# A decoder layer in one kernel: last stores awaited at the next write of their buffers instead of at the stage borders

## The chip, the cores and the metric

The kernel runs on one core of a Trainium2 chip. The metric is the device time of one execution in microseconds, as the median over several runs. The profile comes from one execution of its own. Engine names are those of the profile: PE is TensorE (PEld its weight loads), DVE VectorE, ACT ScalarE, POOL GpSimd, SP the engine that issues most DMAs.

## The reference

One step of a decoder layer, all in float32, for 2048 prompt tokens and 8 sequences of 8 decode tokens (17 tiles of 128 tokens). Cut to what matters here:

```python
mod = silu(c) @ w_ada + b_ada                       # sh1, sc1, gt1, sh2, sc2, gt2
hn = rms_norm(x, g_pre_mix) * (1 + sc1) + sh1
u, q, k, v = split(hn @ w_in, [512, 1024, 1152])    # 512 | 512 | 128 | 128 columns
attn = attn_prompt(q, k, v, sinks, table)           # window 128, 8 heads, 2 kv heads, one sink per head
ssm_y, h_last = s5_scan(u, lam, log_dt, b, c, d)    # 32 groups of 16 channels, complex state of 64
z = gelu(ssm_y); ssm_out = z * sigmoid(z @ w_glu + b_glu)
mixed = concat(rms_norm(ssm_out), rms_norm(attn)) @ w_out
x = x + gt1 * rms_norm(mixed, g_post_mix)
hn2 = rms_norm(x, g_pre_ffn) * (1 + sc2) + sh2
x = x + gt2 * rms_norm(hier_moe(hn2), g_post_ffn)   # top 1 of 4 groups, top 2 of 4 experts
```

The decode tokens run the same with cached keys and values and a given scan state. The outputs are `x`, the last 128 keys and values, and the scan's last states, for both kinds of tokens.

## The kernel before, in words

`hybrid_layer` runs five stages in order. **front** computes the first two modulations and the projection `x @ w_in` for 17 tiles and stores each to `scratch_proj` (`store`, L250 to 252, the counters `stored[0]` for even tiles and `stored[1]` for odd ones); beside it the scan's matrices are built and stored to `scratch_rec` (`store_rec`). Tile 16 (`LAST`) holds the decode tokens and is even. **s5** runs the scan for 32 groups `g`: SP loads each group's matrices into a ring of four (`load_rec`), `u` and `us` (the decode tokens') come from `scratch_proj`, PE, DVE, ACT and POOL work a group in a fixed order of steps (`contribute`, `back`, `unflip` on PE), and `y` goes to `scratch_y` in quarters (`store_y`). Beside the groups runs the second half of the modulation, `modulate(n)` for n of 0 to 15 on PE with `w_ada` loaded by `load_w(n)`, finished by DVE in two parts, `folded` 1 at g = 17 and `folded` 2 behind the last group. Its rows go to `scratch_mods` (`store_rows`, four DMAs from SP, four from ACT), the last states to four outputs (`store_states`, three DMAs from each). **attention** works the tiles in `ORDER`: 0 to 5, the decode tokens "S", 6 to 15, with `q` and `k` in two buffers `held_qk` (tiles 0 and 1 are loaded during s5; `load(t)` waits until tile t - 2 is flipped). Meanwhile POOL runs `MixingWeights.split` (L1299): 48 loads of the modulation's rows for the decode tokens (`mw_mod<-scratch_mods`), then it splits ten weight tiles in two parts for the next stage. **mixing** does gate, norms, output projection and residual for 17 tiles; its SP stores `x` and `hn` and, for each tile, fills one tile of `scratch_acc` with zeros (`clear(t)`, 18 in all). **moe** runs the experts and adds their results into `scratch_acc`.

Every stage is a `with Stage(...)`: its SBUF and PSUM tiles and one block in which each engine has its own instruction list. Orders are written out by hand; there is no planner. At a block's end all five engines meet (their instructions have line L79). Before it, SP (in s5 ACT's list ends with stores too) waits in the old kernel for every store of the stage: in front L326 to 329, in s5 L1049 and L1050 (`stored`, 24 DMAs), in attention L1403, in mixing L1814 to 1817. Buffers of a stage share addresses with those of the next, so a store must have been read out before the next stage writes there.

Semaphores are held by a `Semaphores` object. Its exit is a barrier of all engines (L64), a clear of its counters by POOL (L65) and a second barrier (L66). In the old kernel there are three such groups: front with s5, attention with mixing, and moe. So the first exit stands between s5 and attention.

Of the kernel before, what the change touches and what calls it, by code (L numbers as in the profile page):

```python
# [22 lines left out]
P = 128  # L23
# [14 lines left out]
L = 8  # L38
# [10 lines left out]
class Semaphores:  # L49
# [12 lines left out]

    def __exit__(self, *a):
        self.nc.all_engine_barrier()  # L64
        self.nc.clear_and_free_semaphores(self.held)  # L65
        self.nc.all_engine_barrier()  # L66
# [94 lines left out]
def front(nc, T, top, cT):  # L161

    with Stage(nc, top, "fr") as s:
# [79 lines left out]
        def _(sp):  # L243
# [81 lines left out]
            sp.wait_ge(stored[0], 9 * 16)  # L325
# [209 lines left out]
        def _(dve):  # L535
# [278 lines left out]
            for t in range(NT):  # L814
# [18 lines left out]
                if t == 0:  # L833
                    power_tables()

# [59 lines left out]
class AttentionFirst:  # L895


    def __init__(self, held):
        sb = held.sb
        self.ident, self.sink, self.bias = sb("ident", [P, P]), sb("sink", [P, NH]), sb("bias", [P, NH, 2 * WIN])  # L900
        self.qk = sb("qk", [P, 2, AW + KVW])
        self.arrived, self.kv_stored = held.sem("first"), held.sem("kv_stored")
# [21 lines left out]

U5 = 4


def s5(nc, T, top, cT, first):

    with Stage(nc, top, "s5") as s:  # L930
        ident, swap = first.ident, s.sb("swap", [P, P])
        u, us = s.sb("u", [P, 2, L, SW]), s.sb("us", [DB, L, SW])
        y, ys = s.sb("y", [P, 2, L, SW]), s.sb("ys", [DB, L, SW])
# [8 lines left out]
        fin, fins = s.sb("fin", [NG, P]), s.sb("fins", [P, 2, P])  # L942
        w, mod, gains = s.sb("w", [P, 2, 2048]), s.sb("mod", [P, 2, 512]), s.sb("gains", [P, 2, 512])
# [8 lines left out]
        last_ready, edges, fin_mm, fin_out, stored = (s.sem(n) for n in ("last_ready", "edges", "fin_mm", "fin_out", "stored"))  # L952
# [7 lines left out]
        yp = T["y"][0:SEQ, :].rearrange("(i p j) c -> p i j c", i=2, j=L)  # L960
        ysv = T["y"][SEQ:SEQ + NS, :].rearrange("(b j) c -> b j c", j=L)
# [9 lines left out]

        def store_rows(eng, h):
            for n, row in enumerate((2, 4)):
                a = n * 2 + h
                eng.dma_start(T["mods"][:, row, h * 512:(h + 1) * 512], mod[32 * a:32 * a + NRW, 0, :]).then_inc(stored, 16)
            for a in (2 * h, 2 * h + 1):
                eng.dma_start(T["mods"][:, 3, a * 256:(a + 1) * 256], mod[32 * a:32 * a + NRW, 1, 0:256]).then_inc(stored, 16)

        def store_states(eng, r):
            part, c = ("re", "im")[r], slice(r * NST, (r + 1) * NST)  # L980
            eng.wait_ge(fin_out, 2)
            eng.dma_start(T[f"o_ssm_{part}_prompt"][0, 0], fin[:, c]).then_inc(stored, 16)
            for n in range(2):
                dst = T[f"o_ssm_{part}_sample"].rearrange("a b g p -> (a b g) p")[n * P:(n + 1) * P, :]
                eng.dma_start(dst, fins[:, n, c]).then_inc(stored, 16)

        @blk.sync
        def _(sp):
# [17 lines left out]
            def store_y(b):  # L1006
                sp.wait_ge(y_out, (b + 1) * 8)
                c = slice(b * CB, (b + 1) * CB)
                for i in range(2):
                    sp.dma_start(yp[:, i, :, c], y[:, i, :, c]).then_inc(stored, 16)  # L1010
# [16 lines left out]
            sp.dma_start(T["cT"], cT[:, :, :].rearrange("p k n -> p (k n)")).then_inc(stored, 16)  # L1027
            for g in range(U5, NG):
# [14 lines left out]
            sp.wait_ge(y_out, NG)  # L1043
            sp.dma_start(ysv, ys[:, :, :]).then_inc(stored, 16)
            store_y(3)
            sp.wait_ge(folded, 2)
            store_rows(sp, 0)
            store_states(sp, 0)
            first.finish(sp)  # L1049
            sp.wait_ge(stored, 24 * 16)  # L1050

        @blk.scalar
        def _(act):
# [39 lines left out]
            act.wait_ge(folded, 2)  # L1093
            store_rows(act, 1)
            store_states(act, 1)

        @blk.tensor
        def _(pe):
# [39 lines left out]

            def modulate(n):
# [14 lines left out]
            for g in range(NG):  # L1154
# [8 lines left out]
            pe.wait_ge(mod_done, 2)  # L1163
            pe.wait_ge(edges, 1)
            pe.wait_ge(tail_in, 3 * 16)
            nc.tensor.matmul(ps_f[0:NG, 0:P], lastA[:, :], ident[:, :], start=True, stop=False)
            nc.tensor.matmul(ps_f[0:NG, 0:P], lastB[:, :], swap[:, :], start=False, stop=True)
            for n in range(2):
                last = nc.tensor.transpose(ps_f[:, (n + 1) * P:(n + 2) * P], ss[:, 4 * n:4 * n + 4, :].rearrange("q b g -> q (b g)"), ident[:, :])
            last.then_inc(fin_mm, 1)  # L1170
# [26 lines left out]
        def _(dve):  # L1197
# [53 lines left out]
            modulation(1)  # L1251
            vec.scalar_tensor_tensor(mod[:, 1, 0:256], mod[:, 1, 0:256], 1.0, gains[:, 1, 0:256], ALU.add, ALU.mult).then_inc(folded, 1)
# [5 lines left out]
            vec.tensor_copy(fin[:, :], ps_f[0:NG, 0:P]).then_inc(fin_out, 1)  # L1258
            vec.tensor_copy(fins[:, :, :], ps_f[:, P:3 * P].rearrange("p (n q) -> p n q", n=2)).then_inc(fin_out, 1)
# [4 lines left out]
class MixingWeights:  # L1264
# [34 lines left out]
    def split(self, nc, pool, T):  # L1299

        nc.gpsimd.memset(self.w_rt[:, :, NR:], 0.0).then_inc(self.padded, 1)
# [1497 lines left out]
```

## Time and profile before

| | us |
|---|---|
| median of 3 runs | 1610.88 (1610.49 to 1613.52) |
| the profiled execution | 1611.89 |
| its span | 1610.1 |
| front | 0 to 355.9 |
| s5 | 355.9 to 511.8 |
| attention | 511.8 to 675.4 |
| mixing | 675.4 to 1018.8 |
| moe | 1018.8 to the end |

The stage borders are the first instructions of each stage in the timeline. Over the span PE is busy 84%, DVE 74%, ACT 45% and POOL 33% of the time, and the mean granted clock of PE is 0.92 of full speed. A timeline row gives start, busy time, engine, line, operation and tiles, the count of instructions merged in it, and in brackets how long the engine stood idle before and what released it. SPq, ACTq and PEq are the sequencers of these engines: their rows are DMA issues and waits.

### The profile page before, as it was taken

Reading aid. Unit: us, or ns where it says so; the run is one execution under the profiler, and the core shown is the slowest. Engines: PE = TensorE matmul, PEld = TensorE weight load, DVE = VectorE, ACT = ScalarE, POOL = GpSimd, SP = SyncE. Lnnn points to the kernel's source line nnn. Section 1 sums busy time; section 2 is a strip of 40 time slices with the busy share of each in tenths; the row PEclk is TensorE's granted clock in tenths of the full one; section 3 lists DMA queues with packets and bytes.
Section 4 is the critical chain, followed back from the end, with each engine's and each line's share of the span. In section 5 each row is a group of like instructions: output and inputs, shape, how many; then the busy total and the mean of one; then the engine's idle time right before and its main releaser. Section 6 shows DMA issues by size and latency. Waiting matters only on the chain. (4 is left out here: it accounts for less than half of the span.)

```text
span 1610.1 us, 24720 instructions
## 1 busy us (share of the span) xinstructions
PE 1352.4 (84%) x7108; PEld 1029.4 (64%) x7109; DVE 1185.6 (74%) x2154; ACT 729.7 (45%) x1564; POOL 537.9 (33%) x719
## 2 busy tenths in 40 slices
PE   4899989979996879689999997179999999999910
PEld 1687777856664546467777775157777777777700
DVE  3799898846684767546666664668899888988738
ACT  2321212102342737533444342137777777777633
POOL 1105567642223860012112211134444444444300
PEclk8899999987997979889999998579999999999965
DMA  9412434449986642214433442875788888885597
GB/s 344 144 69 104 156 124 162 178 162 364 333 273 164 193 147 85 100 39 162 163 132 130 158 155 92 280 254 111 198 230 251 261 217 242 250 212 123 114 311 292
DMA packets 139063, 301.08 MB, mean 187 GB/s; under 512 B 22312, under 2 KB 79913, under 8 KB 136246
## 3 DMA queue, kind: packets, MB, share of 16 engines
q1 hardware_dynamic: 110742, 221.06, 39.8%
q0 software_dynamic: 20800, 61.13, 16.4%
q10 hardware_dynamic: 7448, 17.99, 3.2%
q8 instruction: 36, 0.59, 0.2%
q14 instruction: 37, 0.30, 0.1%
HBM read 317.05 MB, written 103.70 MB: 261 GB/s over the span
## 5 line engine op out<-in xcount | busy, mean ns | idle before, releaser
L2569 DVE TENSOR_TENSOR ex_w_lo<-ex_wgu,ex_w_hi 128x1024 fp32r<-128x1024 f32 x192 | 226.2, 1221 | 46.8 <-ACT ex_w_hi L2366 46.6
L2366 ACT ACTIVATE ex_w_hi<-ex_wgu 128x1024 fp32r (+1 forms) x192 | 192.4, 1055 | 42.7 <-issue 23.0
L2329 POOL DMA_INDIRECT scratch_acc<-ex_o,ex_to x48 | 95.9, 1999 | 253.6 <-DVE ex_o L2599 184.1
L116 PE MATMUL ex_ps_h<-ex_w_hi,ex_xT 128*128 128x512 f32 x384 | 156.3, 407 | 2.7 <-DVE ex_x_lo L2563 2.7
L116 PE MATMUL fr_ps_m<-fr_whi,fr_hl 128*128 128x512 f32 (+1 forms) x408 | 150.6, 369 | 7.3 <-DVE fr_io L598 4.4
L118 PE MATMUL ex_ps_h<-ex_w_hi,ex_x_lo 128*128 128x512 f32 x384 | 151.8, 395 | 0.0
L117 PE MATMUL ex_ps_h<-ex_w_lo,ex_xT 128*128 128x512 f32 x384 | 151.1, 393 | 0.0
L117 PE MATMUL fr_ps_m<-fr_wlo,fr_hl 128*128 128x512 f32 (+1 forms) x408 | 148.1, 363 | 0.0
L118 PE MATMUL fr_ps_m<-fr_whi,fr_hl 128*128 128x512 f32 (+1 forms) x408 | 147.5, 361 | 0.0
L1828 POOL TENSOR_SCALAR mx_st<-mx_st 128x1 f32<-128x1 f32 x68 | 29.4, 433 | 267.1 <-ACT mx_j L1872 151.4
L116 PE MATMUL mx_ps_m<-mw_hi,mx_hT 128*128 128x512 f32 x272 | 108.0, 397 | 4.1 <-issue 2.1
L117 PE MATMUL mx_ps_m<-mw_lo,mx_hT 128*128 128x512 f32 x272 | 106.7, 392 | 0.0
L118 PE MATMUL mx_ps_m<-mw_hi,mx_h_lo 128*128 128x512 f32 x272 | 106.6, 392 | 0.0
L2698 PE MATMUL ex_ps_o<-ex_wd,ex_aT 128*128 x192 | 98.0, 591 | 0.0
L116 PEld LDWEIGHTS fr_ps_m<-fr_whi,fr_hl 128*128 128x128 f32 x408 | 79.1, 194 | 22.9 <-DVE fr_io L598 5.3
L118 PEld LDWEIGHTS fr_ps_m<-fr_whi,fr_hl 128*128 128x128 f32 x408 | 79.4, 195 | 11.8
L117 PEld LDWEIGHTS fr_ps_m<-fr_wlo,fr_hl 128*128 128x128 f32 x408 | 79.5, 195 | 11.4
L116 PEld LDWEIGHTS ex_ps_h<-ex_w_hi,ex_xT 128*128 128x128 f32 x384 | 73.2, 191 | 17.2 <-DVE ex_x_lo L2563 2.4
L118 PEld LDWEIGHTS ex_ps_h<-ex_w_hi,ex_x_lo 128*128 128x128 f32 x384 | 72.9, 190 | 16.4
L117 PEld LDWEIGHTS ex_ps_h<-ex_w_lo,ex_xT 128*128 128x128 f32 x384 | 73.5, 191 | 14.2
L409 ACT ACTIVATE fr_hl<-fr_ps_t 128x512 fp32r<-128x512 f32 x34 | 18.5, 595 | 131.0 <-PE fr_ps_t L471 121.2
L1437 ACT ACTIVATE at_sc<-at_sc,at_nm 128x256 f32<-128x256 f32 (+1 forms) x128 | 62.7, 493 | 17.7 <-DVE at_nm L1513 17.7
(454 smaller groups left out, 3388.0 us busy)
## 6 DMA issues: line engine op xcount, KB each, us to landing
ex_wgu<-in_w_exp_gate_dram SPq DMA_DIRECT2D x51, 1024.0 KB, 11.8
ex_wgu<-in_w_exp_up_dram SPq DMA_DIRECT2D x51, 1024.0 KB, 14.7
ex_wd<-in_w_exp_down_dram SPq DMA_DIRECT2D x51, 1024.0 KB, 11.1
scratch_rec<-fr_w SPq DMA_DIRECT2D x16, 1112.0 KB, 5.4
s_rec<-scratch_rec SPq DMA_DIRECT2D x32, 556.0 KB, 6.3
scratch_proj<-fr_io SPq DMA_DIRECT2D x17, 640.0 KB, 3.0
scratch_acc<-in_zeros_dram SPq DMA_DIRECT2D x18, 512.0 KB, 6.0
scratch_x<-mx_x SPq DMA_DIRECT2D x17, 512.0 KB, 2.7
```

The lines of the kernel that those rows point to most:

```text
L116: nc.tensor.matmul(out, hi, w_hi, start=first, stop=False)
L117: nc.tensor.matmul(out, hi, w_lo, start=False, stop=False)
L118: return nc.tensor.matmul(out, lo, w_hi, start=False, stop=final)
L409: A(hi[:, t % 2, 4 * h:4 * h + 4, :], ps_t[:, h, :].rearrange("p (k n) -> p k n", k=4), ACT.Copy).then_inc(moved_a, 1)
L1437: last = A(sc[:, p % 2, h, k0:], sc[:, p % 2, h, k0:], ACT.Exp, bias=nm[:, p % 2, h:h + 1], accum_out=sm[:, p % 2, h:h + 1])
L1828: last = nc.gpsimd.tensor_scalar(a[:, col + m:col + m + 1], a[:, col + m:col + m + 1], c, EPS, ALU.mult, ALU.add)
L2329: pool.indirect_dma_start(T["acc"], bass.IndirectOffsetOnAxis(to[:, t:t + 1], 0), o[:, t % 2, :], None, compute_op=ALU.add).then_inc(sem(" ...
L2366: A(w_hi[:, par, c * PW:(c + 1) * PW], wgu[:, bass.ds(slot * (KD * 2 * DE) + c * PW, PW)], ACT.Copy).then_inc(S["w_rounded"], 1)
L2569: vec.tensor_tensor(w_lo[:, par, c * PW:(c + 1) * PW], wgu[:, bass.ds(slot * (KD * 2 * DE) + c * PW, PW)], w_hi[:, par, c * PW:(c + 1) * P ...
L2698: last = nc.tensor.matmul(ps_o[:, at], aT[:, 1, :], wd[:, bass.ds((slot * 2 + 1) * D + c * 512, 512)], start=False, stop=True)
```

## The change

- **Front** no longer waits for the last even store (`stored[0]` 8 instead of 9 DMAs). s5 makes that wait before it loads `us`, which now comes behind `load_u(0)`.
- **s5**: an object `ScanResults` holds the tiles that are stored late, with one counter `scan_stored`. Four of the stores of modulation rows (the two rows that are complete at `folded` 1) are issued by SP at g = 21. The four matmuls for the last states come before the last `unflip` on PE and write to `s_ps_s`, and DVE takes them before its last modulation part. The thirteen stores at the stage's end are gone from both lists; SP waits only for `cT` and the cache copies.
- **Attention**: SP issues these thirteen behind `v` and tile 2, which moves up. POOL waits for all 23 before it writes the weights' tiles. POOL clears the counters of front and s5 behind its first two weight loads, without barriers.
- **Attention to mixing**: the last odd tile's store is awaited in mixing, by SP ahead of its loop and by ACT.
- **Mixing**: the zero fills `clear(LAST)` and `clear(NT)` come ahead of the loop.
- Counters: `early` (front, s5) and `late` (attention, mixing, and the held ones) instead of one group per pair of stages.

```diff
@@ Semaphores
+    def clear(self):
+        self.nc.clear_and_free_semaphores(self.held)
...
@@ front, SP
-            sp.wait_ge(stored[0], 9 * 16)
+            sp.wait_ge(stored[0], 8 * 16)
@@ ScanResults
+    def store_gate_and_shift(self, sp, T):
+        for n, row in enumerate((2, 4)):
+            for h in range(2):
+                a = n * 2 + h
+                sp.dma_start(T["mods"][:, row, h * 512:(h + 1) * 512], self.mod[32 * a:32 * a + NRW, 0, :]).then_inc(self.stored, 16)
+
+    def store_rest(self, sp, T):
+        for a in range(4):
+            sp.dma_start(T["mods"][:, 3, a * 256:(a + 1) * 256], self.mod[32 * a:32 * a + NRW, 1, 0:256]).then_inc(self.stored, 16)
+        self.store_y(sp, T, 3)
+        sp.dma_start(T["y"][SEQ:SEQ + NS, :].rearrange("(b j) c -> b j c", j=L), self.ys[:, :, :]).then_inc(self.stored, 16)
+        for r, part in enumerate(("re", "im")):
...
+    def all_stored(self, eng):
+        eng.wait_ge(self.stored, 23 * 16)
@@ s5, SP
-            sp.dma_start(us[:, :, :], usv).then_inc(loaded, 16)
             sp.dma_start(ident[:, :], T["ident"]).then_inc(loaded, 16)
             load_u(0)
+            sp.wait_ge(proj_stored, (NT // 2 + 1) * 16)
+            sp.dma_start(us[:, :, :], usv).then_inc(loaded, 16)
...
+                if g == 21:
+                    sp.wait_ge(folded, 1)
+                    res.store_gate_and_shift(sp, T)
...
-            sp.wait_ge(y_out, NG)
-            sp.dma_start(ysv, ys[:, :, :]).then_inc(stored, 16)
-            store_y(3)
-            sp.wait_ge(folded, 2)
-            store_rows(sp, 0)
-            store_states(sp, 0)
+            sp.wait_ge(cT_out, 16)
             first.finish(sp)
-            sp.wait_ge(stored, 24 * 16)
@@ s5, ACT
-            act.wait_ge(folded, 2)
-            store_rows(act, 1)
-            store_states(act, 1)
@@ s5, PE
+                if g == NG - 1:
+                    last_states()
                 unflip(g)
@@ MixingWeights.split, POOL
+        first.results.all_stored(pool)
         nc.gpsimd.memset(self.w_rt[:, :, NR:], 0.0).then_inc(self.padded, 1)
...
         self.load_raw(pool, T, 1)
+        early.clear()
@@ attention, SP
             sp.dma_start(v[:, :, :], pv[:, 0:NPT, AW + KVW:]).then_inc(v_in, 16)
+            load(2)
+            first.results.store_rest(sp, T)
...
-                sp.wait_ge(tile_out[t], NPT // 2 * 16)
+                sp.wait_ge(tile_out[t], (NPT // 2 - t) * 16)
@@ mixing, SP
+            clear(LAST)
+            clear(NT)
+            sp.wait_ge(m.attn_stored, NPT // 2 * 16)
             run(sp, step, HALF - 2)
             store(Tile(0, LAST))
             sp.wait_ge(S["kept"], 32)
-            clear(LAST)
-            clear(NT)
@@ mixing, ACT
             round_z(Tile(0, 0))
+            act.wait_ge(m.attn_stored, NPT // 2 * 16)
             square_attn(Tile(0, 0))
@@ hybrid_layer
+        with Semaphores(nc) as late, Stage(nc, late, "held") as held:
...
+            proj_stored = front(nc, T, early, cT)
...
+                attention(nc, T, late, mw, first, early)
+                mixing(nc, T, late, mw, lg)
```

How the lists move at three places. SP from the end of s5 to the start of attention, before (`s_` tiles are s5's, `at_` attention's; L79 is the border):

```order
L1044 DMA scratch_y<-s_ys 8x4096
L1010 DMA scratch_y<-s_y 1024x1x128 x2
L975 DMA scratch_mods<-s_mod 9x512 x2
L977 DMA scratch_mods<-s_mod 9x256 x2
L982 DMA out_ssm_re_prompt_dram<-s_fin 32x64
L985 DMA out_ssm_re_sample_dram<-s_fins 128x64 x2
L79 UNCONDITIONAL_BRANCH
L1360 UNCONDITIONAL_BRANCH
L1374 DMA at_v<-scratch_proj 128x16x128
L1376 DMA at_s_hsel<-in_hsel_dram 8x256
L1377 DMA at_s_sink_c<-in_attn_sinks_dram 8x1
L1378 DMA at_s_qkv<-scratch_proj 64x768
```

and with the change (the border is L83 now):

```order
L83 UNCONDITIONAL_BRANCH
L1384 UNCONDITIONAL_BRANCH
L1398 DMA at_v<-scratch_proj 128x16x128
L1388 DMA held_qk<-scratch_proj 128x640
L954 DMA scratch_mods<-s_mod 9x256 x4
L944 DMA scratch_y<-s_y 1024x1x128 x2
L956 DMA scratch_y<-s_ys 8x4096
L959 DMA out_ssm_re_prompt_dram<-s_fin 32x64
L962 DMA out_ssm_re_sample_dram<-s_fins 128x64 x2
L959 DMA out_ssm_im_prompt_dram<-s_fin 32x64
L962 DMA out_ssm_im_sample_dram<-s_fins 128x64 x2
L1402 DMA at_s_hsel<-in_hsel_dram 8x256
```

The stage's stores stand behind the border, and tile 2 ahead of them. PE at the end of s5, before:

```order
L1127 MATMUL s_ps_v<-s_B,s_rec 128x256
L1130 MATMUL s_ps_v<-s_A,s_rec 128x264
L1136 MATMUL s_ps_y<-held_ident,s_yT 128x128 x2
L1137 MATMUL s_ps_y<-held_ident,s_yT 8x128
L1147 MATMUL s_ps_f<-s_w,held_cT 32x256 x4
L1166 MATMUL s_ps_f<-held_ident,s_lastA 32x128
L1167 MATMUL s_ps_f<-s_swap,s_lastB 32x128
L1169 MATMUL s_ps_f<-held_ident,s_ss 128x128 x2
L79 UNCONDITIONAL_BRANCH
```

and with the change:

```order
L1145 MATMUL s_ps_v<-s_B,s_rec 128x256
L1148 MATMUL s_ps_v<-s_A,s_rec 128x264
L1160 MATMUL s_ps_s<-held_ident,s_lastA 32x128
L1161 MATMUL s_ps_s<-s_swap,s_lastB 32x128
L1163 MATMUL s_ps_s<-held_ident,s_ss 128x128 x2
L1154 MATMUL s_ps_y<-held_ident,s_yT 128x128 x2
L1155 MATMUL s_ps_y<-held_ident,s_yT 8x128
L1174 MATMUL s_ps_f<-s_w,held_cT 32x256 x4
L83 UNCONDITIONAL_BRANCH
```

The products with `s_lastA`, `s_lastB` and `s_ss` no longer follow the modulation (`s_w`) but precede the last unflip. POOL at the start of attention, before (the two ISA rows, L65 in both, are the clears of counters):

```order
L79 UNCONDITIONAL_BRANCH
L65 ISA
L1405 UNCONDITIONAL_BRANCH
L1301 MEMSET mw_w_rt 128x8x12
L131 DMA mw_mod<-scratch_mods 8x1024 x48
L1295 DMA at_raw<-in_w_glu_dram 128x2x512 x2
```

and with the change:

```order
L83 UNCONDITIONAL_BRANCH
L1430 UNCONDITIONAL_BRANCH
L1323 MEMSET mw_w_rt 128x8x12
L135 DMA mw_mod<-scratch_mods 8x1024 x48
L1316 DMA at_raw<-in_w_glu_dram 128x2x512 x2
L65 ISA x2
```

The clear leaves the border and stands behind the first weight loads.

## Rows read from the trace of the kernel before

**Rows 1.** Windows: stretch, us, busy of each engine (instructions), clock, DMA share, GB/s.
```profile
500.00:512.00 12.00, 1.17 (x7) 0.79 (x8) 1.49 (x5) 0.00 (x0) 0.18 (x1) 0.63 0.49 120
512.00:525.00 13.00, 9.49 (x53) 6.83 (x53) 4.90 (x31) 6.27 (x22) 12.77 (x25) 0.68 1.00 223
```
**Rows 2.** SP's waits, 330 to 372 us: total, times, longest.
```profile
SPq L79 <- DMA scratch_proj<-fr_io: 1.4, 1, 1.4
```
**Rows 3.** Timeline, start of s5.
```profile
365.20 0.42 ACT L1062 ACTIVATE s_ug<-s_u 128x256 f32<-128x256 f32 x1 [22.12 <-DMA s_u<-scratch_proj]
...
369.31 0.69 PE L1108 MATMUL s_ps_u<-held_ident,s_ug 128*128 128x128 f32 x2
```
**Rows 4.** Timeline, s5 around the ring load of group 22.
```profile
449.70 1.31 SPq L1010 DMA_DIRECT2D scratch_y<-s_y  x2
...
451.92 2.87 SPq L992 DMA_DIRECT2D s_rec<-scratch_rec  x1
...
459.68 0.68 PE L1118 MATMUL s_ps_s<-s_uT,s_rec 128*128 128x264 f32 x2 [0.88 <-issue]
```
**Rows 5.** Timeline, end of s5 and first product of attention.
```profile
498.78 0.64 PE L1147 MATMUL s_ps_f<-s_w,held_cT 128*32 128x256 f32 x8
...
499.44 0.30 SPq L1044 DMA_DIRECT2D scratch_y<-s_ys  x1
...
499.95 0.42 DVE L1252 SCALAR_TENSOR_TENSOR s_mod<-s_mod,s_gains 128x256 f32<-128x256 f32 x1
...
500.40 0.55 ACTq L975 DMA_DIRECT2D scratch_mods<-s_mod  x1
...
502.02 0.40 DVE L1259 COPY s_fins<-s_ps_f 128x256 f32<-128x256 f32 x1
...
505.51 0.97 ACTq L985 DMA_DIRECT2D out_ssm_im_sample_dram<-s_fins  x2
...
506.32 0.93 SPq L985 DMA_DIRECT2D out_ssm_re_sample_dram<-s_fins  x2
...
511.80 1.09 PE L1577 MATMUL at_ps_q<-held_ident,held_qk 128*128 128x128 f32 x4 [10.02 <-PEq L66]
```
**Rows 6.** Lines L1050 and L65: count, ns min/median/max, first and last start.
```profile
L1050 SPq EVENT_SEMAPHORE  x1: 28/28/28, 509.4 to 509.4; - x1
...
L65 POOLq EVENT_SEMAPHORE_RANGE_CLEAR  x3: 524/591/657, 510.5 to 1609.2; - x3
```
**Rows 7.** DMA issues, 512 to 540 us: count, KB each, median us from issue to landing.
```profile
held_qk<-scratch_proj SPq DMA_DIRECT2D x4, 320.0 KB, 8.5
```
**Rows 8.** Timeline, attention's first tiles (SP's loads of tiles 3 and 4, PE's first products).
```profile
518.80 0.34 SPq L1364 DMA_DIRECT2D held_qk<-scratch_proj  x1
...
524.21 0.63 PE L1577 MATMUL at_ps_q<-held_ident,held_qk 128*128 128x128 f32 x4 [0.73 <-DMA held_qk<-scratch_proj]
...
529.79 0.58 SPq L1364 DMA_DIRECT2D held_qk<-scratch_proj  x1
...
530.83 0.44 PE L1577 MATMUL at_ps_q<-held_ident,held_qk 128*128 128x128 f32 x2
...
538.52 0.66 PE L1577 MATMUL at_ps_q<-held_ident,held_qk 128*128 128x128 f32 x4
```
**Rows 9.** PE's granted clock at attention's start (window of PE), and POOL's first row of mixing.
```profile
512.00:513.00 1.00, 1.00 (x5) 0.50 0.09 28
...
675.44 0.10 POOL L1819 MEMSET mx_half<- 128x2 f32 x1 [83.01 <-POOLq L79]
```
**Rows 10.** Line L1403, SP's last wait of attention.
```profile
L1403 SPq EVENT_SEMAPHORE  x1: 1628/1628/1628, 673.4 to 673.4; - x1
```
**Rows 11.** SP's waits, 1000 to 1030 us, and the timeline's last row of mixing.
```profile
SPq L79 <- DMA scratch_acc<-in_zeros_dram: 2.7, 1, 2.7
SPq L1814 <- DMA scratch_hn<-mx_hn: 2.1, 1, 2.1
...
1014.55 0.18 DVE L1986 TENSOR_TENSOR kept_lg<-mx_ps_g,mw_b_rt 128x20 f32<-128x20 f32 x1 [2.22 <-PE mx_ps_g L2092]
```

More of the change, by code:

```diff
@@ L61, in get @@
         return self.held[-1]
+    def clear(self):
+        self.nc.clear_and_free_semaphores(self.held)
     def __exit__(self, *a):
         self.nc.all_engine_barrier()
-        self.nc.clear_and_free_semaphores(self.held)
+        self.clear()
         self.nc.all_engine_barrier()
@@ L834, in _ @@
                     power_tables()
+        return stored[0]
 BW = 3 * WIN
@@ L901, in __init__ @@
         self.qk = sb("qk", [P, 2, AW + KVW])
-        self.arrived, self.kv_stored = held.sem("first"), held.sem("kv_stored")
+        self.arrived, self.kv_stored, self.scan_stored = held.sem("first"), held.sem("kv_stored"), held.sem("scan_stored")
     def load_tiles(self, sp, T):
@@ L970, in cols @@
             return slice(g * GC, (g + 1) * GC)
[L972 to L985, printed above, removed]
         @blk.sync
@@ L1137, in unflip, with last_states @@
                 nc.tensor.transpose(ps_y[0:DB, 2 * P:3 * P], yT[:, g % 2, NCH:], ident[:, :]).then_inc(y_flipped, 1)
+            def last_states():
+                pe.wait_ge(edges, 1)
+                pe.wait_ge(tail_in, 3 * 16)
+                nc.tensor.matmul(ps_s[0:NG, 0, 0:P], lastA[:, :], ident[:, :], start=True, stop=False)
+                nc.tensor.matmul(ps_s[0:NG, 0, 0:P], lastB[:, :], swap[:, :], start=False, stop=True)
+                for n in range(2):
+                    last = nc.tensor.transpose(ps_s[:, 0, (n + 1) * P:(n + 2) * P], ss[:, 4 * n:4 * n + 4, :].rearrange("q b g -> q (b g)"), ident[:, :])
+                last.then_inc(fin_mm, 1)
             def modulate(n):
@@ L1162, in _ @@
                     modulate(g // 2)
[L1163 to L1170, printed above, removed]
         @blk.gpsimd
@@ L1297, in load_raw, with split @@
             pool.dma_start(dst, T["w_out"][0, (k - 2) * P:(k - 1) * P, :]).then_inc(arrived, 16)
-    def split(self, nc, pool, T):
+    def split(self, nc, pool, T, first, early):
+        first.results.all_stored(pool)
         nc.gpsimd.memset(self.w_rt[:, :, NR:], 0.0).then_inc(self.padded, 1)
@@ L1324, with attention @@
 HEADS = [[kv * GQ + 2 * half + g for kv in range(NKV) for g in range(2)] for half in range(2)]
-def attention(nc, T, top, mw, first):
+def attention(nc, T, top, mw, first, early):
     NB = 2 * NKV
@@ L1379, in _ @@
             sp.dma_start(s_vn[:, :, :], new[:, SW + AW + KVW:].rearrange("(b t) c -> t b c", t=DT)).then_inc(s_loaded, 16)
-            load(2)
             for kv in range(NKV):
@@ L1406, in _ @@
         def _(pool):
-            mw.split(nc, pool, T)
+            mw.split(nc, pool, T, first, early)
         @blk.scalar
@@ L2752, in hybrid_layer @@
         T[name] = nc.dram_tensor(f"scratch_{name}", shape, dt).ap()
+    early = Semaphores(nc)
     with Stage(nc, None, "kept") as kept:
         lg = kept.sb("lg", [P, NT, NR])
-        with Stage(nc, None, "held") as held:
-            with Semaphores(nc) as top:
-                held.top = top
-                cT = held.sb("cT", [P, KD, 32])
-                front(nc, T, top, cT)
-                first = AttentionFirst(held)
-                first.spare = cT
-                s5(nc, T, top, cT, first)
-            with Semaphores(nc) as top:
-                with Stage(nc, top, "mw") as weights:
-                    mw = MixingWeights(weights)
-                    attention(nc, T, top, mw, first)
-                    mixing(nc, T, top, mw, lg)
+        with Semaphores(nc) as late, Stage(nc, late, "held") as held:
+            cT = held.sb("cT", [P, KD, 32])
+            proj_stored = front(nc, T, early, cT)
+            first = AttentionFirst(held)
+            first.spare = cT
+            s5(nc, T, early, cT, first, proj_stored)
+            with Stage(nc, late, "mw") as weights:
+                mw = MixingWeights(weights)
+                attention(nc, T, late, mw, first, early)
+                mixing(nc, T, late, mw, lg)
         with Semaphores(nc) as top:
```

45 lines of the change are left out of this document (29 added, 16 removed).

## The prediction

> **What bounds it now.** The printed chain of waits reaches back only into the last stage, so the borders had to be read one by one. First the windows [rows 1] show where the program stands still: in 500 to 512 us PE works 1.17 us of 12 and the DMA engines are half busy; the 13 us behind it have the DMA engines at 1.00 and 223 GB/s. Then the queue engine's own waits show which border waits for what [rows 2, 6, 10, 11], and the timeline shows what stands ahead of each border and behind it. Four places count: front to s5 (A), s5 to attention (B), attention to mixing (C), mixing to the experts (D).
>
> **A, minus 1.35.** Once the scan matrices' stores have landed, SP ends front with 1.4 us more for the last store of the projection [rows 2]. The second wait goes. It is made again in s5 behind the first load of `u`, some 2 us after the border; by then the 1.4 us have run out, so it should be met on arrival. The load of `us` behind it comes about 1 us later. Its readers: ACT gathers `u` and `us` from 365.20 (until 365.8), PE flips the first group only at 369.31, after the bias products [rows 3]. Some 3.5 us cover it. Bounds: 1.2 to 1.4.
>
> **s5 at g = 21, plus 0.5.** Four stores of 18 KB now stand on SP ahead of the ring load for group 22. SP waited there with 0.9 us to spare (its store of `y` was done at 451.01, the ring load went out at 451.92), and four issues at 0.33 (the quick ones of its queue) are 1.3. So the load goes out 0.4 late, and PE is already short of it: 0.88 us idle at 459.68, whose cause the row does not name [rows 4]. At the pace of the same stores at the stage's end (0.55 for the first of them, [rows 5], over 1 for the others) it would be 2, if the ring makes it up it is 0.
>
> **B, minus 10.7.** Last real work before it: PE's modulation ends at 499.42, DVE's fold at 500.37, then the last states on PE and two copies until 502.42. The stores run from 499.44 to 507.25 on SP (ten) and from 500.40 to 506.48 on ACT (seven) [rows 5]. SP's wait for them ends at 509.4, and the barrier, 0.657 us clear, barrier bring PE's first attention product to 511.80 [rows 5, 6]. In the changed program the states come before the last unflip, so DVE's fold ends the stage. PE's unflip moves by four small matmuls, of which part lies in PE's waits: 0.3, so DVE ends near 500.65. Stage A's own rendezvous took about 0.4 from the last branch to the first instruction. Attention starts near 501.05: 511.75 less that is 10.7. If the modulation waits for the copies too it is 10.0, if unflip does not move it is 11.1. Nothing of what was waited for sits on PE's path: the first two tiles were loaded during s5.
>
> **The start of attention, plus 1.6.** The stores don't vanish, they go into SP's list behind `v` and tile 2. Before, counted from attention's first instruction (SP's at 511.75, just ahead of PE's in [rows 5]), tile 3's load was issued at +7.05 and wanted at +19.1, tile 4's issued at +18.0 and wanted at +26.8; such a load landed in 8.5 [rows 7, 8]. Thirteen more issues, eleven at 0.35 and the two halves of `y` at 0.65 [rows 4], are 5.2, so tile 3 goes out at +12.2 and lands at +20.7: **1.6 late**. Tile 4's load stands behind three copies that wait for the eight bias loads; it moves by 0 to 5.2. At 0 it lands at +26.5 and is in time, at 5.2 it lands at +31.7, when the want has itself moved to +28.4: 3.3 late; I take the middle, **1.7**, because both ends have a reason. For the early one: POOL waits for all 23 stores before its 48 loads of 32 KB (1.5 MB), which before began at once and filled the queues [rows 1]. Sum of stalls 3.3; the ends are 0 (rival 1) and those of rivals 2 and 3. Against that stands the clock: at the stage's start the granted clock was 0.50, level 1.2 GHz, after PE's 10.02 us of idle [rows 5, 9]; without that idle I expect the 2.4 GHz level. Four transposes took 1.09 at the low level and 0.63 later [rows 5, 8]. The first 13 us hold some four such groups' worth of transposes, 0.46 each: **minus 1.7** (0 if the clock falls all the same; 9.49 busy us at 0.68 [rows 1] give 3.0 at most). That is plus 1.6.
>
> What hides the rest: POOL's weights were done 83.0 us before mixing wanted POOL [rows 9], and the wait for the stores costs it some 15. The two clears on POOL now lie inside attention and cost 1.1 of that same cover. Without it they would be 1.1 on the path.
>
> **C, minus 1.6.** SP's wait for the last attention store was 1.628 us [rows 10]; now only the even tiles are awaited, which have landed. Who reads it next is mixing, and there both new waits come later than the store's landing, 1.6 us after SP's issue: SP's stands behind eleven issues at the stage's start, and ACT's ahead of the first square of the attention half, which cannot start before that tile's own loads are in. The two zero fills moved ahead of the loop meet an SP that is idle for some 16 us before its next load at 696.4. Cost nothing; 0.5 if they slow the loads under way.
>
> **D, minus 1.1.** SP's last wait was for the second zero fill: 2.7 us, of which the `hn` store ahead had run out 2.1 us into its own wait [rows 11]. With the fills moved, the stage ends with DVE at 1014.73 or the `hn` store at 1014.3, not at 1017.0 [rows 11]: minus 2.2. But the counters of this group lie apart now and the clear is three instructions for one. A clear takes 0.591 us in the median [rows 6], 0.55 as the two extra ones follow without a drain: plus 1.1, on the path, for every engine stands at the second barrier. **The end, plus 1.1:** the last group's clear also falls into three. Bounds of both: 0, if the clears pipeline, to 1.3.
>
> **Sum.** −1.35 + 0.5 − 10.7 + 1.6 − 1.6 − 1.1 + 1.1 = −11.55. The profiled execution took 1611.89 (span 1610.1), so 1600.3; it stood 1.0 above the median of the runs, 1610.88, so 1599.3 on their scale. I round to **1599.0**.
>
> **Rival 1, no stall at all (17%).** SP issues at 0.35 and the queues stay short since POOL holds back: tile 3 lands in 6, not 8.5, tile 2, issued 3.5 us earlier, removes the 0.73 wait for it [rows 8], and the clock stays up. Then −13.15 for the terms outside attention, −1.7 and −0.7: −15.55, 1595. For it: POOL's 1.5 MB are gone from the crowded stretch. Against it: the DMA share there was 1.00 and the stores bring 1.3 MB (two halves of 0.52, `ys` 0.13, the states 0.15).
>
> **Rival 2, the loads stand behind the stores' bytes (15%).** 1.3 MB at the 223 GB/s of that stretch are 5.8 us. If tile 3 lands in 8.5 + 5.8 instead of 8.5, it comes at +26.5, 7.4 late, and with tile 4's 1.7 the stalls are 9.1 instead of 3.3: −5.75, 1605. What would do it here: the queue serves what was issued first. The Trainium skill (DMA: Bandwidth & Descriptors, "Queues, rings and completion order") says so of the counter: its increment lands only after every earlier write of that DMA engine, across its queues. By that rule alone the time would be rival 2's. The trace does not settle it: 8.5 us for 320 KB behind 1 MB of `v` [rows 7] fits the rule and mere sharing alike.
>
> **Rival 3, slower (4%).** SP issues the stores as slowly as the stage's end did, when they took 7.8 on SP and 6.1 on ACT at once [rows 5]: 13.9 in one list, and SP works alone now. Tile 3 goes out at +21, lands at +29.5, 10.4 late, and tile 4 another 3.3. PE stands still each time and comes back at 0.50: two tiles at some 2 us more. 17.7 in all against −13.15 of the other terms: plus 4.5, 1615. It decides once attention's start is worse by over 16.3. Against it: the slow issues were two engines' at once and with full queues; single ones on SP take 0.30 to 0.34 [rows 5, 8].
>
> **Rival 4, it doesn't do what it says (4%).** Another wait ends last at B (SP's for the cache copies, POOL's or ACT's branch) and most of the 10.7 comes back: 1608 to 1611, within 0.2%.
>
> **Numbers.** 0.2%, about what a measurement of this kernel can tell, is 3.2 us. The forecast has 60%, its own terms reach from −17 to −8. The range takes in rivals 1 and 2: 1594 to 1606. Slower by over 0.2% is rival 3, 4%; the same is rival 4 and a corner of rival 2 with slow issues, 6%; the rest, 90%, is faster.
>
> **What would show it.** A: s5's first instruction at about 354.6, and no wait of SP for the projection in s5. B: attention's first product near 499 to 500 on the new scale, less than 1 us of PE idle ahead of it, a granted clock of 1.00 in its first us. Tile 3's load issued at about +12 and PE waiting for it 1 to 2 us; SP issuing thirteen stores in 4 to 7 us. POOL starting its 48 loads some 14 us into attention, done with 60 us to spare. C: mixing starts within 0.5 us of the last attention store's issue. D: three clears in a row, 1.7 us. The forecast is wrong if PE waits over 5 us for tile 3 or 4, if attention (163.6 us before) gets longer by over 4, or if s5's groups behind 21 run slower.

## The result, and the profile after

The changed kernel took 1592.57 us in the median of 4 runs (1590.79 to 1596.33), the kernel before 1610.68 in its 4; the ratio is 0.9894, with a 95% interval from 0.9869 to 0.9918. That is 18.1 us (13.2 to 21.1) where 12 were forecast, and 1592.57 lies below the range. In a later comparison of the same two kernels (after_again, below) the ratio was 0.9884 (0.9854 to 0.9915).

The profiled execution of the changed kernel took 1590.79 us, 21.1 less than the one before. By stage, from the first instruction of each:

| | before | after | difference | forecast |
|---|---|---|---|---|
| front, up to its last projection store | 351.24 | 348.85 | −2.4 | 0 |
| that store to s5's first load (A) | 4.68 | 3.37 | −1.3 | −1.35 |
| s5, first load to DVE's last fold | 144.03 | 146.72 | +2.7 | +0.8 |
| that fold to attention's first load (B) | 11.80 | 0.71 | −11.1 | −11.0 |
| attention, first load to the last at_o | 160.51 | 154.79 | −5.7 | +1.6 |
| at_o to mixing's first operation (C) | 3.18 | 1.58 | −1.6 | −1.6 |
| mixing, up to its last logits | 339.11 | 340.74 | +1.6 | 0 |
| logits to the experts' first load (D) | 4.26 | 2.13 | −2.1 | −1.1 |
| the experts, to the span's end | 591.29 | 590.11 | −1.2 | +1.1 |

The borders did what they were meant to do. Front's −2.4 is the luck of two profiles: over all that were taken its means are 350.3 us with the old borders (six) and 350.1 with the new ones (eight). The page's head:

```profile
span 1589.0 us, 24710 instructions
...
PE 1350.5 (85%) x7108; PEld 1029.8 (65%) x7109; DVE 1176.2 (74%) x2154; ACT 728.7 (46%) x1564; POOL 534.7 (34%) x719
```

The same 2154 instructions of DVE are busy 1176.2 us instead of 1185.6. Nothing in the change should make DVE faster; that is the first trace of what the forecast had missed.

The timeline around B and the first tiles, which answers to [rows 5] and [rows 8]:

```profile
498.94 0.42 DVE L1280 SCALAR_TENSOR_TENSOR s_mod<-s_mod,s_gains 128x256 f32<-128x256 f32 x1
499.65 0.38 SPq L1398 DMA_DIRECT2D at_v<-scratch_proj  x1
...
499.69 0.63 PE L1602 MATMUL at_ps_q<-held_ident,held_qk 128*128 128x128 f32 x4 [1.27 <-PEq L83]
...
502.04 1.61 SPq L954 DMA_DIRECT2D scratch_mods<-s_mod  x4
...
503.69 1.26 SPq L944 DMA_DIRECT2D scratch_y<-s_y  x2
505.00 1.83 SPq L956 DMA_DIRECT2D scratch_y<-s_ys  x1
...
509.93 0.89 SPq L962 DMA_DIRECT2D out_ssm_im_sample_dram<-s_fins  x2
...
515.73 0.35 SPq L1388 DMA_DIRECT2D held_qk<-scratch_proj  x1
...
520.06 0.92 PE L1602 MATMUL at_ps_q<-held_ident,held_qk 128*128 128x128 f32 x4 [3.71 <-DMA held_qk<-scratch_proj]
...
521.15 0.58 SPq L1388 DMA_DIRECT2D held_qk<-scratch_proj  x1
```

PE is idle 1.27 us at the border where it was 10.02, and its first four transposes take 0.63 us where they took 1.09. Thirteen stores take SP from 502.04 to 510.82, 8.8 us and not 5.2, so tile 3's load goes out at +16.1 (forecast +12.2); but it lands in 4.3 us, not 8.5, and PE starts on it at +20.4 after 3.71 us of waiting. The window of PE that answers to [rows 9], and the two wide ones that answer to [rows 1] (500 to 513 and 513 to 526):

```profile
500.00:501.00 1.00, 0.42 (x4) 1.00 0.15 30
```
```profile
500.00:513.00 13.00, 9.01 (x62) 5.84 (x60) 5.68 (x34) 8.82 (x31) 1.01 (x3) 0.87 0.78 215
513.00:526.00 13.00, 9.29 (x61) 6.69 (x61) 6.45 (x30) 6.60 (x24) 13.00 (x27) 0.87 0.90 214
```

The granted clock is at full speed in attention's second us. The DMA share is 0.78 where it was 1.00, and POOL, whose loads filled that stretch before, has hardly begun (fifth pair: 1.01 us busy). The counters' clears, which answer to [rows 6], and SP's waits before D, which answer to [rows 11]:

```profile
L65 POOLq EVENT_SEMAPHORE_RANGE_CLEAR  x8: 46/254/415, 538.4 to 1588.5; - x8
```
```profile
SPq L1840 <- DMA scratch_hn<-mx_hn: 3.5, 1, 3.5
```

Eight clears have a median of 0.254 us, where three had 0.591. The wait for a zero fill is gone; SP's last one there is for the store of `hn`.

### The profile page after: what moved, and what is told of

Read it like the earlier page. It is cut to its first block and busy times, and to the rows that moved or that the text cites. A ratio compares the mean times of both kernels' runs of the same rounds, so it can differ in the third digit from the quotient of the medians.

```text
span 1589.0 us, 24710 instructions
## 1 busy us (share of the span) xinstructions
PE 1350.5 (85%) x7108; PEld 1029.8 (65%) x7109; DVE 1176.2 (74%) x2154; ACT 728.7 (46%) x1564; POOL 534.7 (34%) x719
## 5 line engine op out<-in xcount | busy, mean ns | idle before, releaser
L2349 POOL DMA_INDIRECT ex_x<-scratch_hn,ex_rows x48 | 52.4, 1092 | 52.5 <-DVE ex_rows L2569 25.6
```

The lines of the kernel that those rows point to most:

```text
L2349: pool.indirect_dma_start(x[:, t % U, :], None, T["hn2"], bass.IndirectOffsetOnAxis(rows[:, t:t + 1], 0)).then_inc(S["x", t % U], 16)
```

## What made attention shorter

DVE's groups in attention, kernel before and after (line, operation, shape, count, busy us, mean ns, idle before). Before:

```profile
L1513 DVE SCALAR_TENSOR_TENSOR at_nm<-at_mx,at_nsink 128x4 f32<-128x4 f32 x32 | 8.5, 266 | 1.1
L1532 DVE TENSOR_TENSOR at_sm<-at_sm,at_es 128x8 f32<-128x8 f32 x16 | 7.2, 451 | 0.0
...
L1502 DVE SCALAR_TENSOR_TENSOR at_nm<-at_mx,at_s_nsink 128x2 f32<-128x2 f32 x2 | 2.5, 1264 | 0.2
L1493 DVE TENSOR_SCALAR at_s_nsink<-at_s_sink 128x4 f32<-128x4 f32 x1 | 2.3, 2304 | 0.0
```

After:

```profile
L1538 DVE SCALAR_TENSOR_TENSOR at_nm<-at_mx,at_nsink 128x4 f32<-128x4 f32 x32 | 7.1, 223 | 1.1
...
L1557 DVE TENSOR_TENSOR at_sm<-at_sm,at_es 128x8 f32<-128x8 f32 x16 | 3.5, 219 | 0.0
L1527 DVE SCALAR_TENSOR_TENSOR at_nm<-at_mx,at_s_nsink 128x2 f32<-128x2 f32 x2 | 2.7, 1372 | 0.2
...
L1518 DVE TENSOR_SCALAR at_s_nsink<-at_s_sink 128x4 f32<-128x4 f32 x1 | 0.2, 171 | 0.0
```

Operations of 2 to 8 columns take 0.16 us, and now and then over 2. One such meeting, in the timeline of the kernel before, and the same operation in that of the changed one:

```profile
562.26 2.35 POOL L1310 TENSOR_TENSOR mw_lo<-at_raw,mw_hi 128x1024 fp32r<-128x1024 f32 x1
562.37 2.26 DVE L1532 TENSOR_TENSOR at_sm<-at_sm,at_es 128x8 f32<-128x8 f32 x1
```
```profile
550.70 0.30 DVE L1557 TENSOR_TENSOR at_sm<-at_sm,at_es 128x8 f32<-128x8 f32 x1
...
551.05 2.36 POOL L1333 TENSOR_TENSOR mw_lo<-at_raw,mw_hi 128x1024 fp32r<-128x1024 f32 x1
```

The small one of DVE starts 0.11 us after POOL's subtraction and ends with it, at 564.6. In the changed kernel's profile the subtraction starts 0.05 us behind the end of DVE's. That need not be the change's doing: in a second profile of the kernel before (before_again, below) the same operation took 0.24 us. I call **excess** what the small operations of DVE in attention (`at_nm`, `at_sm`, `at_ds`, `at_s_nsink`) take above 0.162 us each: 13.9 us before, 5.4 after. The difference, 8.5, is close to what attention lost from tile 5's first product (at +34.24 before, at +36.81 after) to the start of its last `at_o`: 126.3 and 118.0, so 8.3. (The expectations below count attention to the end of that `at_o`, 0.7 later: 161.2 and 155.5.) The large operations that read PSUM (the copies, `at_o`) have the same mean, 0.69 us, in both. The Trainium skill has this rule (SBUF — State Buffer, "Who interferes with whom"): POOL and DVE share a pair of ports as an exclusive lock, and a DVE instruction with two inputs in SBUF, or in a two-port mode, contends for it with a POOL instruction that reads SBUF; the second to come waits the first one out. These rows agree: `at_sm` has two SBUF inputs and ended with POOL's subtraction.

Two theories then. **Theory 1:** it is these meetings, and POOL's later start only deals them anew. **Theory 2:** the later start takes POOL's loads out of the crowded first us, or the clock does it. They don't exclude each other.

## The experiments

**b_quarters: the kernel before, POOL's pieces a quarter as long.**

```diff
-            nc.gpsimd.tensor_copy(self.hi[:, k, :], self.raw[:, k % 2, :]).then_inc(self.rounded, 1)
...
+            for c in range(4):
+                c4 = slice(c * D // 4, (c + 1) * D // 4)
+                nc.gpsimd.tensor_copy(self.hi[:, k, c4], self.raw[:, k % 2, c4]).then_inc(self.rounded, 1)
+                pool.wait_ge(self.rounded, 4 * k + c + 1)
+                nc.gpsimd.tensor_tensor(self.lo[:, k, c4], self.raw[:, k % 2, c4], self.hi[:, k, c4].bitcast(F32), ALU.subtract).then_inc(self.rest, 1)
+                pool.wait_ge(self.rest, 4 * k + c + 1)
```

> The kernel before, with the ten rounding copies and ten subtractions that POOL makes during the attention each cut in four pieces of 256 columns. Theory 1 (the attention got shorter because DVE's small operations on SBUF tiles no longer have to wait out POOL's 2.35 us subtractions): a piece lasts some 0.6 us, so the 13.9 us that the small ones of DVE (sums, negated maxima, the decode tokens' sinks) take above their 0.16 each fall to about 4, and the attention's 161.2 us up to its last at_o by 6 to 10, to about 153; whole kernel 6 to 10 faster than before. Theory 2 (it got shorter because POOL's 48 loads no longer crowd the start, or by the clock): no change of attention, within 1 us, POOL some 3 us later.

Measured: ratio 0.9967 (0.9941 to 0.9992), 1608.44 against 1612.92. The excess fell from 13.9 to 4.6, attention from 160.5 to 156.1 us: as far as theory 1 from tile 5 on (126.3 to 116.2), but tiles 3 and 4 came later this time (tile 4's product at +32.4 instead of +26.8), where PE waited 3.6 us for their loads and only 0.7 in the first profile of the kernel before. The gain of 4.5 us is less than the 6 to 10 expected.

**a_quarters: the same cut in the changed kernel.**

> The changed kernel with the same cut. Theory 1: 5.4 us of excess are left in it, of which some 3 to 4 go; attention 155.5 to 152, and the difference to the cut kernel before shrinks from 18 to about 12, which is what the borders bring. Theory 2: no change against the changed kernel (18 faster than before), and 18 against the cut kernel before.

Measured: ratio 0.9892 (0.9862 to 0.9921), 1593.55 against 1612.92. Excess 4.0, attention 150.2 (154.8 uncut). Between the two cut kernels lie 14.9 us, between the uncut ones 18.1 and 20.7: theory 1's direction, 3 to 6 less where I expected 6 less. With four runs of one of the two cut kernels that shrinkage is not clear of the noise.

**b_split_late and b_pool_held: POOL later, in the kernel before.** The first holds only the splitting, the second all of POOL's list:

```diff
         for k in range(2 + KD):
+            if k == 0:
+                pool.wait_ge(flipped, 6)
```
```diff
+            pool.wait_ge(k_flipped, 3)
             mw.split(nc, pool, T)
```

> The kernel before, with POOL's loads where they were, but its first rounding copy held until PE has flipped the sixth tile's keys (39 us into the attention, 9 us later than before, 2 earlier than in the changed kernel). Theory 1: other operations of DVE meet other ones of POOL; the excess changes from 13.9 by several us (I expect less, 3 to 9, for the decode tokens' step had the longest meetings), the attention by the same. Theory 2: no change, since the loads crowd the start as before.

> The kernel before, with all of POOL's list in the attention held until the third flip (15 us), about as the wait for the stores holds it in the changed kernel. Theory 1: excess between 4 and 10, attention shorter by the difference. Theory 2: attention shorter by the same 6 to 8 as in the changed kernel, with the excess no smaller in proportion; tile 3 and 4 land in 6 us instead of 8.5.

Measured: 0.9998 (0.9981 to 1.0014) and 0.9963 (0.9945 to 0.998). b_split_late: excess 10.4, 3.5 less, and attention 159.1, 1.4 less; a miss by size, and its total shows nothing. b_pool_held: excess 10.8, attention 157.8, tile 5's product at +33.9. Its loads of `q` and `k`, to be read beside [rows 7] (issues, 510 to 538 us):

```profile
held_qk<-scratch_proj SPq DMA_DIRECT2D x4, 320.0 KB, 4.1
```

Against the first profile of the kernel before (+34.2) that start shows no gain, but that profile was an unusually quick one. In the five profiles with POOL's loads at the start (before, before_again, b_clears3, b_split_late, b_quarters) such a load landed in 8.5 to 11.1 us, PE waited 0.7, 1.1, 5.2, 3.1 and 3.6 us in all for them, and tile 5's product came at +37.7 in the mean. With POOL's list held they landed in 4.1, PE did not wait at all, and the kernel was 6.8 us (3.2 to 8.9) faster in the median; holding the splitting alone, with the loads left where they were, brought nothing. So theory 2's gain is there, and the excess of 10.8, the same as the kernel before has in the mean (below), doesn't explain it. Where in the kernel all of the 6.8 lie, one profile does not tell: its attention is 1.9 below the mean of three.

**a_barriers: two barriers back at B, no clear, stores deferred.**

```diff
             s5(nc, T, early, cT, first, proj_stored)
+            nc.all_engine_barrier()
+            nc.all_engine_barrier()
```

> The changed kernel with the two barriers back between s5 and attention, without a clear between them and with the stores still deferred. Before, DVE's last fold to SP's first attention load took 11.8 us in every profile of an old border (four of them), now 0.7. If the stores were nearly all of it, the two barriers add 1.3 to 2.0 here (509.5 to 511.75, less the 0.66 of the clear): border 2.0 to 2.7, whole kernel plus 1.5. If barriers are dear in themselves (each wakes five engines, PE's clock falls behind them), border over 4 and the clock of attention's first us below 1.00.

Measured: 1594.72 against 1609.97. The border took 1.36 us instead of 0.71 (the fold at 497.23, the first load at 498.59), below my 2.0 to 2.7; PE's granted clock was at full speed from 500 to 502 us. Two barriers on idle engines are 0.65. The same profile has the excess at 10.7 and attention at 161.2 us, with not one instruction of attention altered.

**a_stores_in_s5: the thirteen stores back at the end of s5, on SP, awaited.**

```diff
             sp.wait_ge(cT_out, 16)
+            sp.wait_ge(folded, 2)
+            sp.wait_ge(fin_out, 2)
+            sp.wait_ge(y_out, NG)
+            res.store_rest(sp, T)
             first.finish(sp)
+            res.all_stored(sp)
```

> The changed kernel with its thirteen late stores back at the end of s5 on SP alone, and awaited there; no barriers, no clear. Border: 13 issues in 5 to 9 us, then 2.2 until landing: 8 to 11 us instead of 0.7. In attention tile 3's load goes out 5 to 8 us earlier and PE's 3.7 us wait for it goes; POOL starts some 15 us earlier, so its subtractions meet other operations of DVE. Sum with the excess unchanged (5.4): plus 5 to 8. If the meetings fall as in the kernel before (13.9): plus 13 to 16.

Measured: 1606.42 against 1609.97, ratio 0.9959 (0.9935 to 0.9982). The border took 10.46 us, 9.75 more than with the stores deferred; but the kernel before issued its stores on two engines, so the two borders are better compared from the end of SP's last wait for stores. From the fold to there it took 9.5 us before (509.4) and 10.0 here (508.7), and from there to attention's first load 2.3 and 0.5. The second difference, 1.8, is the barriers with the clear. So of the 11.8 before the stores were some 9.3, barriers and clear 1.8, and 0.7 is the fold and the rendezvous that stay. SP's waits there:

```profile
SPq L1073 <- DVE s_mod L1285: 1.2, 1, 1.2
SPq L965 <- DMA out_ssm_im_sample_dram<-s_fins: 1.1, 1, 1.1
```

It is the issuing, 499.20 to 507.56, that is long, and the landing only 1.1. PE's wait for tile 3 was gone (product at +18.7), and the excess was 12.0.

**a_fills_last: the zero fills back at the end of mixing.**

```diff
-            clear(LAST)
-            clear(NT)
             sp.wait_ge(m.attn_stored, NPT // 2 * 16)
...
             sp.wait_ge(S["kept"], 32)
+            clear(LAST)
+            clear(NT)
```

> The changed kernel with the two zero fills back behind the last store of mixing. From mixing's last operation of DVE to the first load of the experts: 2.13 us now, 4.3 in the kernel before. Theory A (the fills were all of it, and three clears cost no more than one): back to 4.1 to 4.4, plus 2.2. Theory B (three clears cost 0.5 each more, as I had reckoned, and the 2.13 hides something else): 5 or more.

Measured: 1595.38 against 1609.97. From the last logits to the experts 5.36 us instead of 2.13. By the number alone that is theory B's, but the second fill landed later here, 3.3 us behind the start of the last logits and not 2.5. From its landing to the experts' first load are 2.1 us, against 1.7 in the kernel before: 0.35 for two further clears, not 0.5 each.

**b_clears3: the same counters in more clears.**

```diff
-        self.nc.clear_and_free_semaphores(self.held)
+        n = len(self.held) // 3
+        for part in (self.held[:n], self.held[n:2 * n], self.held[2 * n:]):
+            self.nc.clear_and_free_semaphores(part)
```

> The kernel before with each group's counters cleared in parts: 3 instructions at the first border, 5 before the experts, 8 at the end, where there was one each; the same counters in all. If a clear has a fixed price near its 0.59 us: the three exits last 1.2, 2.4 and 4.1 us longer. If its time goes by the counters that it clears (after the change three took some 1.0 together, one of before 0.66 and its drain 0.23): each exit longer by under 0.5.

```profile
L67 POOLq EVENT_SEMAPHORE_RANGE_CLEAR  x16: 46/131/243, 511.1 to 1610.6; - x16
```

Sixteen clears of 0.131 us in the median. Before the experts SP waited 1.5 us for the barrier behind five of them, 0.9 behind one and, in the changed kernel, 1.3 behind three. Added up, the five take 0.68 us and the one 0.52: a clear's time goes mostly by what it clears, and each further instruction adds 0.15 to 0.2. It was run once, so its total says little (1613.1).

**after_again, before_again: both kernels unaltered, a second profile each.**

> The changed kernel unaltered, for a second profile of it. Theory 1 says its attention length is set by what POOL's subtractions happen to meet: from the start of tile 4's first product to the last at_o the profiles so far follow about 110.5 us plus 1.1 times the excess of DVE's small operations (13.9: 126.3; 10.7: 122.9; 8.2: 121.9; 5.4: 118.0; 4.0: 114.4). If the meetings are chance, this profile's excess differs from 5.4 (I expect 6 to 11, since 5.4 was drawn in the fastest of four runs) and the length follows the line. If the excess is a fixed property of the changed kernel, it is 5.4 again.

> The kernel before unaltered, for a second profile. If the meetings are chance: excess between 8 and 14, attention's length by the same line. If it is a property of this order of the work: 13.9 again. s5 from its first load to DVE's last fold: 144.0 to 146.4, which tells how far single profiles of the same code lie apart.

Measured: the changed kernel 1590.62 against 1611.31, the kernel before 1612.53. Excess 7.5 after (5.4 in the first profile) and 10.5 before (13.9). So it is neither a fixed property nor small. One operation shows it best, `at_s_nsink` in the kernel before, 2304 ns in its first profile and this in its second:

```profile
L1493 DVE TENSOR_SCALAR at_s_nsink<-at_s_sink 128x4 f32<-128x4 f32 x1 | 0.2, 170 | 0.0
```

Over the fourteen profiles, the time from tile 5's first product to the last `at_o` against the excess:

| kernel | excess | us | | kernel | excess | us |
|---|---|---|---|---|---|---|
| before | 13.9 | 126.3 | | a_barriers | 10.7 | 122.9 |
| before_again | 10.5 | 120.1 | | a_fills_last | 8.2 | 121.9 |
| b_clears3 | 8.4 | 119.0 | | after_again | 7.5 | 118.0 |
| b_pool_held | 10.8 | 123.9 | | after | 5.4 | 118.0 |
| b_split_late | 10.4 | 124.4 | | a_stores_in_s5 | 12.0 | 125.7 |
| b_quarters | 4.6 | 116.2 | | a_stores_last | 12.8 | 124.7 |
| a_quarters | 4.0 | 114.4 | | a_best | 2.4 | 116.2 |

A line through them has a slope of about 1.0 and starts at 112; the points lie within 3 us of it. By this line attention pays in full what DVE waits for POOL, whichever kernel it is. Where attention and POOL's pieces are unaltered, the three profiles of the old border have 13.9, 10.5 and 8.4 (mean 10.9), the four of the new one 5.4, 7.5, 8.2 and 10.7 (mean 7.9).

**a_stores_last: the stores behind tile 3's load.**

```diff
             load(2)
-            first.results.store_rest(sp, T)
...
             load(3)
+            first.results.store_rest(sp, T)
```

> The changed kernel with the thirteen late stores behind tile 3's load in SP's list instead of behind tile 2's. Theory: PE's 3.7 us wait for tile 3 is the thirteen issues (15.73 against 7.05 us before) and nothing else; the load goes out near +9, PE's wait falls under 0.5, tile 4's load may be 1 to 3 late instead; POOL starts some 4 us later, which the 66 us of cover take. Minus 2 to 3 at tile 5's start (36.8 now), plus or minus 4 by what POOL meets. Rival: the bytes matter, not the place in the list, and then tile 4 waits as long as tile 3 did: no gain.

Measured: 1593.94 against 1611.31. Tile 3's load went out at 506.73 (+7.0), PE's wait for it is gone and tile 5's product came at +32.8 instead of +36.8, tile 4 without a wait: the 3.7 us were the place in the list. But this profile had an excess of 12.8, attention was 157.5 us, and the median is no better than the changed kernel's.

**a_best: the stores behind tile 3's load, and POOL's pieces an eighth as long.**

```diff
+            for c in range(8):
+                c4 = slice(c * D // 8, (c + 1) * D // 8)
```

> Both remedies: the late stores behind tile 3's load, and POOL's rounding copies and subtractions in eight pieces each. Quarters took 0.73 us a piece and left an excess of 4.0; eighths should take 0.45 and leave about 2.5, POOL still done 20 us before mixing. Attention 160.5 in the kernel before, 154.8 changed, 150.2 with quarters: about 147 here. Whole kernel: 20 to 23 faster than before, 3 to 5 faster than the changed one. If pieces cost DVE more meetings than they shorten, it is no better than quarters (19 faster).

Measured: 1585.13 against 1611.31, ratio 0.9838 (0.9808 to 0.9868), and 1590.62 for the changed kernel in the same comparison. 26.2 us faster than before, more than the 20 to 23 expected; the 5.5 over the changed kernel come from five and six runs whose times overlap.

```profile
L1335 POOL TENSOR_TENSOR mw_lo<-at_raw,mw_hi 128x128 fp32r<-128x128 f32 x80 | 36.4, 456 | 6.4
```
```profile
649.87 0.10 POOL L1847 MEMSET mx_half<- 128x2 f32 x1 [18.68 <-POOLq L83]
```

The subtractions cost POOL 36.4 us instead of 23.6, and it is still done 18.7 us before it is wanted. Excess 2.4, attention 149.15 us (147 expected).

## Why the prediction was wrong

Direction and main mechanism held: the gain is at B, 11.1 us in the profile. The size did not, and single profiles cannot tell by how much. Means over the profiles do it better (old border: before, before_again and the b kernels; new border: after, after_again and the a kernels, each where the stretch is unaltered):

- **A, −1.35: right**, −1.3, with SP waiting only for the scan matrices' store; the wait made again in s5 was met on arrival. One profile of each border has a slower store of these matrices, and 6.2 and 4.9 there.
- **s5 at g = 21, +0.5, and unflip, +0.3: not there.** From s5's first load to DVE's last fold the six profiles of the old border have a mean of 145.4 us (144.0 to 146.4) and the eight of the new one 145.4 (144.2 to 146.7). The profile that the forecast read was the shortest of the old ones.
- **B, −10.7 with that 0.3 in it: right**, −11.1. It is stores 9.3 and barriers with clear 1.8.
- **The start of attention, +1.6: a step that failed.** Issues took 8.8 us and not 5.2, the landing 4.3 and not 8.5; by luck both errors nearly cancel, and tile 5 started 2.6 later than in [rows 8]'s profile. The 8.5 is the median of loads in the crowded first us, with 1 MB of `v` and POOL's 48 beside them; tile 3's went out at +16 and took half of that although POOL had begun 3.6 us earlier, and in b_pool_held, without POOL's, the early ones took 4.1. And [rows 8]'s profile was quick. The kernel before has tile 5's product at +34.2, +38.2 and +41.3 in three profiles (in the last PE waited 4.0 for tile 4), the changed one at +36.7 to +38.3 in four: −0.8 and not +1.6. Of the clock's 1.7 (four times 0.46 would be 1.8) 1.4 show at once: the second tile's product came at +2.4 instead of +3.8, and at +3.1 in after_again.
- **"What hides the rest: POOL's weights": the other step that failed.** I priced POOL's wait at nothing since POOL has time to spare (66.1 us are left, some 68 forecast). It has; but a later POOL is itself a gain. In the kernel before, holding its list for 15 us was worth 6.8 us (3.2 to 8.9), with the loads of `q` and `k` landing in half the time. Besides, POOL's work stands in DVE's way wherever it lies. The mean excess differs by 3.0 us between the two kernels, and the time behind tile 5's first product by 1.6 (121.8 and 120.2); whether that is the change's own or the luck of three and four profiles, these runs do not settle. Between the cut kernels, where little is left to meet, the gain is 14.9.
- **C, −1.6: right**, −1.60.
- **D, −1.1, and the end, +1.1: mis-sized.** Two further clears were priced at 0.55 each, and are 0.15 to 0.2 each. D brought 2.3 in the mean (4.4 to 2.1), and the end, from the last landing to the last instruction, cost 0.3 (1.84 and 2.14). The rest of the experts' −1.2 is scatter: their means are 590.5 and 590.2.
- **Zero fills ahead of the loop, nothing: perhaps 0.8.** Mixing up to its last logits has means of 339.6 and 340.4, with single profiles from 338.8 to 341.4.

With these the sum is −1.3 − 11.1 − 2.4 (attention's 159.7 to 157.3, means of three and four) − 1.6 + 0.8 − 2.3 + 0.3 = −17.6, against the measured −18.1. Against the forecast's −11.55 that is 2.0 more at D and the end, 0.9 more in s5 and B, 4.0 more in attention (2.4 of them before tile 5's product, 1.6 behind it), and 0.8 less in mixing. The attention part is the largest, and the least certain: it rests on three and four profiles that lie up to 7 us apart. Rival 3 (slow issues) was half right: SP took 8.8 us, not the 13.9 it had, and PE waited 3.7. Rival 2 (tile 3's load behind the stores' bytes) did not come about: POOL, which waits for all of the stores, began its loads at 512.1, so they had landed 3.6 us before that load went out at 515.73. It landed in 4.3, but whether a load with 1.3 MB of stores ahead of it waits for them, this does not tell. Rival 1 came nearest by its number (1595), and its shorter landing was right (4.3 us, where it had 6); but it had no stall at all, and there was one. Rival 4 is out as well: nothing else ended last at B.

## What to carry to other kernels

A store that only the next reader needs can be awaited there; what it saves is mostly the issuing at the border, so look first at what the deferred issues now stand ahead of, and put them behind the first load that is wanted. Before calling an engine's work covered, ask what else it holds while it runs. Here POOL's 48 small loads in the crowded first us doubled the landing time of the loads that PE wanted next, and its subtractions of 2.35 us cost DVE up to 2.3 for an operation of 0.16; cutting them in eight and moving the stores took the median 5.5 us below the changed kernel's. Terms of 1 to 3 us should come from several profiles: identical code differed by 2.4 us in s5 and 7 at the start of attention.

## What the runs showed of the hardware

- SP's first four loads of 320 KB in attention landed in 4.1 us (median) with POOL's 48 loads of 32 KB held back for 15 us, and in 8.5 to 11.1 with these from the start. The fourth landed in 4.2 us although POOL's loads were under way again by then, so it is the crowd of the first us and not POOL's loads alone.
- A DVE operation of 8 columns on SBUF tiles that starts just behind a POOL subtraction ends with it (2.26 us for 0.16). DVE's operations of 512 columns that read PSUM kept their 0.69 us in both kernels.
- A clear of counters has no fixed 0.6 us: 0.591 in the median for three that cover each group in one, 0.131 for sixteen that cover the same ones.
- Two barriers of all engines with nothing between them cost 0.65 us; with the 0.66 us clear of POOL between them, 1.8.
- PE came out of a 1.27 us pause with its clock at full speed, and out of one of 10.02 us at half.
